# The third mixer of a two-block transformer kernel: value chunks ahead of query and key, with 1/rms spread inside the first query chunk

## What is computed

```python
# end of the first block
x = rmsnorm(x, final_norm_g)
# start of the second block
h = rms_norm(x, g_pre_mix)
proj = h @ w_in
mq, mk, mv, rq, rk, rv, rg = jnp.split(proj, SPLIT_POINTS, axis=-1)
mq = rotary(split_heads(mq, MOBA_HEADS), moba_inv, ROPE_DIM)
mk = rotary(split_heads(mk, MOBA_HEADS), moba_inv, ROPE_DIM)
mo = merge_heads(moba_attention(mq, mk, split_heads(mv, MOBA_HEADS)))
```

## Time and profile before

| | us |
|---|---|
| median of 3 runs | 1480.52 (1479.03 to 1480.96) |
| profiled execution | 1478.86 |
| its span | 1477.0 |
| PE busy | 1452.9 |
| DVE busy | 828.9 |
| ACT busy | 687.7 |
| POOL busy | 43.2 |
| DMA | 177 GB/s over the span |

### The profile page before, as it was taken

One profiled execution on the slowest core, in us unless ns is written; L12 is line 12 of the kernel. 1 busy time (PEld: TensorE's weight loads), 2 busy tenths in 40 slices (PEclk: granted clock), 3 DMA queues, 4 the chain that ended last, 5 costly groups with the idle time before them and its releaser, 6 DMA issues.

```text
span 1477.0 us, 18731 instructions
## 1 busy us (share of the span) xinstructions
PE 1452.9 (98%) x7412; PEld 1224.2 (83%) x7412; DVE 828.9 (56%) x927; ACT 687.7 (47%) x899; POOL 43.2 (3%) x96
## 2 busy tenths in 40 slices
PE   8999999999999999999999999999999999899997
PEld 6888889988888888888888788888787989788886
DVE  5655565865454555455666464554865565554454
ACT  6545445454444544435445455444544444544442
POOL 1000000000000000000000000000100100000000
PEclk9999999999999999999999999999999999999999
DMA  9755554445555455554444346455433543255551
GB/s 356 260 193 189 181 177 166 171 154 213 178 196 190 152 203 196 189 184 169 171 143 143 114 173 254 174 197 180 176 115 114 189 168 143 100 199 199 181 191 57
DMA packets 38574, 262.14 MB, mean 177 GB/s; under 512 B 4288, under 2 KB 4544, under 8 KB 7648
## 3 DMA queue, kind: packets, MB, share of 16 engines
q1 hardware_dynamic: 37152, 252.85, 48.4%
q0 software_dynamic: 1344, 8.16, 1.4%
HBM read 259.95 MB, written 1.05 MB: 177 GB/s over the span
## 4 chain that ended last, share of the span: by engine, by line
PE 95%; ACT 1%; DVE 1%; SPq 1%; DMA 1%; issue 0%; POOL 0%; POOLq 0%; DVEq 0%; ACTq 0%
PE prod L1001 15%; PE prod L1003 15%; PE prod L1002 15%; PE acc L1001 9%; PE acc L1003 9%; PE acc L1002 9%; PE prod L995 4%; PE prod L996 4%; PE prod L997 4%; PE acc L1168 2%; PE aux L1031 2%; PE acc L1018 1%; DMA raw<-in_weights_dram 1%; PE acc L1187 1%; PE o_bank L1220 1%; ACT acts_h L1319 0%
## 5 line engine op out<-in xcount | busy, mean ns | idle before, releaser
L1489 DVE TENSOR_TENSOR w_lo<-raw,w_hi 128x2048 fp32r<-128x2048 f32 x235 | 538.2, 2291 | 341.3 <-ACT w_hi L1301 341.1
L1301 ACT CAST w_hi<-raw 128x2048 fp32r<-128x2048 f32 x235 | 448.0, 1907 | 293.6 <-PE acc L1003 177.3
L1001 PE MATMUL prod<-w_hi,acts_h 128*128 128x512 f32 x944 | 375.9, 398 | 2.5 <-DVE w_lo L1497 1.7
L1003 PE MATMUL prod<-w_hi,acts_l 128*128 128x512 f32 x944 | 368.8, 391 | 0.0
L1002 PE MATMUL prod<-w_lo,acts_h 128*128 128x512 f32 x944 | 368.4, 390 | 0.0
L1001 PE MATMUL acc<-w_hi,mix_h 128*128 128x512 f32 x600 | 236.7, 395 | 0.3 <-DVE small L1581 0.3
L1003 PE MATMUL acc<-w_hi,mix_l 128*128 128x512 f32 x600 | 233.8, 390 | 0.0
L1002 PE MATMUL acc<-w_lo,mix_h 128*128 128x512 f32 x600 | 233.5, 389 | 0.0
L1001 PEld LDWEIGHTS prod<-w_hi,acts_h 128*128 128x128 f32 x944 | 177.8, 188 | 42.9 <-issue 7.0
L1003 PEld LDWEIGHTS prod<-w_hi,acts_l 128*128 128x128 f32 x944 | 177.5, 188 | 37.7
L1002 PEld LDWEIGHTS prod<-w_lo,acts_h 128*128 128x128 f32 x944 | 177.9, 188 | 35.1 <-issue 0.5
(11 more groups left out here) (255 smaller groups left out, 1220.9 us busy)
## 6 DMA issues: line engine op xcount, KB each, us to landing
raw<-in_weights_dram SPq DMA_DIRECT2D x235, 1024.0 KB, 4.9
raw<-in_weights_dram SPq DMA_DIRECT2D x12, 256.0 KB, 6.6
work<-in_mem_dram POOLq DMA_DIRECT2D x2, 1024.0 KB, 13.4
grow<-in_gain_rows_dram POOLq DMA_DIRECT2D x4, 512.0 KB, 4.4
tabs<-in_tabs_dram POOLq DMA_DIRECT2D x1, 1696.0 KB, 9.4
work<-in_x_t_dram SPq DMA_DIRECT2D x4, 256.0 KB, 6.3
x_res<-in_x_dram SPq DMA_DIRECT2D x1, 1024.0 KB, 8.7
work<-in_mem_t_dram POOLq DMA_DIRECT2D x1, 1024.0 KB, 14.4
```

The lines of the kernel that those rows point to most:

```text
L1001: pe.matmul(out, still_hi, wh, start=first, stop=False, skip_group_check=True)
L1003: return pe.matmul(out, still_lo, wh, start=False, stop=last, skip_group_check=True)
L1301: act.copy(w_hi[:, c % RING], raw[:, c % RAW]).then_inc(hi_done, 1)
L1489: dve.tensor_tensor(w_lo[:, c % RING], raw[:, c % RAW], w_hi[:, c % RING].bitcast(F32), ALU.subtract).then_inc(lo_done, 1)
```

## The change

The third mixer begins with the two value chunks. They are still opened in the middle, with nothing between the halves. The query chunk follows, now opened, with the spread of 1/rms in its middle; then the memory preparation; then the key chunk with the rotation of the query in its middle; then the second query chunk with the rotation of the key in its middle, where heads 0 to 3 are marked ready. The slot behind that chunk is the first that makes scores; before, it was the one ahead of that chunk. Everything from the second key chunk on is written as before.

```diff
--- before.py
+++ after.py
@@ -586,16 +586,13 @@
             pl.ready(units)
         return go
 
-    pl.project(w, 0, "q", 0)
-    pl.project(w, 512, "k", 0, mid=lambda: pl.spread("x"))
+    pl.project_tokens(w, 1024, "v", 0, mid=lambda: None)
+    pl.ready_v(moba)
+    pl.project(w, 0, "q", 0, mid=lambda: pl.spread("x"))
     pl.mem_prep("g_mem", [4, 5, 6, 7], [8, 9, 10, 11], "mem2")
-    pl.rope("q", 0, "moba", pl.read - 1)
-    k_read = pl.read
-    pl.project_tokens(w, 1024, "v", 0, mid=lambda: None, between=lambda: pl.rope("k", 0, "moba", k_read))
-    pl.ready(moba[0:4])
-    pl.ready_v(moba)
-    end(slot)
-    pl.project(w, COLS, "q", 2, mid=slot)
+    q_read = pl.read
+    pl.project(w, 512, "k", 0, mid=lambda: pl.rope("q", 0, "moba", q_read))
+    pl.project(w, COLS, "q", 2, mid=roped_slot("k", 0, "moba", pl.read, moba[0:4]))
     end(slot)
     pl.project(w, 512 + COLS, "k", 2, mid=roped_slot("q", 2, "moba", pl.read))
     end(slot)
```

## The result

| | before | after |
|---|---|---|
| median of 22 runs each | 1479.25 us (1477.89 to 1480.96) | 1481.20 us (1477.76 to 1483.87) |
| profiled execution | 1478.86 | 1483.29 |
| its span | 1477.0 | 1481.5 |
| mean granted clock | 0.995 | 0.992 |

The ratio is 1.0014, with a 95% interval of 1.0008 to 1.0021: some 2 us slower, and within the 0.2% that were set as the bound. The medians differ by 2.0 us, the two profiled executions by 4.4. The instruction rows tell which part of that is the change.

What follows compares the result with a forecast made beforehand. TensorE, busy 98% of the span, was taken as the bound: -2.72 (old waits) + 3.1 (new wait) - 0.4 (switches) + 1.2 (clock) = +1.2 us, added to the median 1480.52 for 1481.7 us; range 1478.6 to 1484.0.

Steps and rivals of the forecast that it cites:

- What bounds it: Start of the third mixer: three PE waits of 0.19, 1.69 and 0.84 us, together 2.72, are all the change can remove directly.
- The hold of POOL: POOL's 1/rms chain: a step issued during DVE's w_lo ends with it; 1/rms at 1053.0 to 1053.3, against 1050.64 before.
- Opening as the cause: At v1: opening this chunk flushes k0's split ahead of v1's scaling on DVE, w_lo running from 1049.6 to 1051.9.
- The wait that takes the place of the old one: Ahead of q0: PE waits 3.1 us for its product bank, until DVE has scaled v's first half with 1/rms.
- The clock: Behind q0's wait: PE's granted clock likely falls to 0.50 for 3.4 us, costing 1.2 us (0 to 2.4).
- Switches: Between chunks and scores: two switches fewer and two waits fewer save 0.4 us (0 to 0.8).
- Rotations and scores: From q0's end to the first scores: DVE side 13.1 us, PE 13.6, so both rotations are ready 0.5 us early.
- rival C: DVE's queue between q0's end and the first scores is late; scores wait up to 2.3 us, 1484.0 us; chance 0.13.
- B: POOL isn't held in mid-chain: 1/rms at 1051.1, PE waits 1.75 us ahead of q0, 1479.1 to 1480.3 us; chance 0.20.
- D: 1/rms arrives under the value chunks and no wait replaces the old ones: -3.1 us, 1477.4 us; chance 0.06.

Runs made afterwards that it cites:

- own bank: Changed kernel, but q0's product goes to the idle accumulator bank acc3, not the product bank holding v's first half; 0.9976 of before, 1476.58 us median.
- the unopened kernel: Changed kernel, but the two value chunks are not opened in the middle; ran once, 1482.88 us.
- the later scores alone: Old order, but the slots behind the value chunk and in the middle of q2 are left out; ratio to before 0.9989.

## Why the prediction was right

The forecast was +1.2 us and a change of under 0.2%; measured were +2.0 at the median (0.14%), +1.7 in the stretch. The mechanism was the one forecast: the old waits went, and a longer one came ahead of q0, by the hold of POOL and the product bank. That the time of 1481.2 lies so near the 1481.7 that was given is in part luck: the step was too small by 0.5 to 0.8 us, and the median before came out 1.3 lower over 22 runs than over 3, so that the two misses took each other back.

Point by point:

* **What bounds it.** PE's waits, 2.72 us in all. Right in the main: taking all of them away (own bank) gave 3.38 us, 0.66 more. A wait costs more than its bracket says. In the earlier trace rows the last matmul ahead of the spread starts at 1048.74 and the spread at 1050.70, 1.96 us later; the bracket says 1.69 and a step at full speed is 0.12, so 0.15 us come on top. The first steps behind a wait are longer as well. Over the three waits PE's rows give some 0.6 us, an estimate.
* **The hold of POOL.** Right in place and size. 1/rms was to come 2.4 to 2.7 us later than before; after the first matmul it came at 1054.47 - 1040.09 = 14.38 instead of 1050.64 - 1038.73 = 11.91, so 2.47. Of these, 0.54 are the later first step (1049.29 - 1040.09 = 9.20 against 1047.39 - 1038.73 = 8.66) and 1.92 the hold. A w_lo that starts between two steps of the chain had no row then; now it has. The rule of the Trainium skill that was weighed there (GPSIMD Engine Reference, section Specifications) is borne out by the 2.11, 2.10 and 0.19 us of the same step.
* **Opening as the cause.** Wrong as a reason, with no effect on the sum: an unopened value chunk does the same, since each engine does the splits that are due when it reaches a chunk, before its own part.
* **The wait that takes the place of the old one.** 3.1 predicted, 3.34 measured. The chain to q0 was right: 15.31 us after the first matmul (1055.40 - 1040.09), where 1054.0 - 1038.73 = 15.27 was reckoned. PE was through v0 and v1 sooner, at 1055.40 - 3.34 = 1052.06, 11.97 after the first matmul and not 12.2, mostly since I charged the turning of x too high (1.0 for 0.79, the step from 1042.84 to 1043.63).
* **The clock.** 1.2 taken, 1.45 in the profiled execution, 2.7 in another execution with the same wait (the unopened kernel). This term was mis-sized: I thought a third of the slow stretch would lie in the wait, and all of it lay behind. The bound of 2.4 was too low for a single execution.
* **Switches.** -0.4 taken. 1.69 = -2.72 + 3.34 + 1.45 - 0.38 leaves 0.38 for them in the changed kernel, but that is a remainder; the later scores alone saved nothing beyond their wait. By the estimate above (some 0.6 us beside three brackets before, some 0.2 beside the one after) it goes with the waits that went, not with the slots: of the term's two reasons, switches fewer and waits fewer, the second holds.
* **Rotations and scores.** 0.5 us of room was reckoned; DVE's second rotation ended 0.15 us ahead of the first scores (1075.60 + 0.69 against 1076.44). They didn't wait, but rival C was nearer than I thought.
* **Rivals.** B fell (the hold is there), C didn't come. B's reasoning that DVE would still have to finish its split first was sound: by the estimate above, the wait without the hold would have been 3.34 - 1.14 = 2.2 us, where B had 1.75. D, the full gain, was reckoned at -3.1; it exists (-3.4), but needs the bank, which the change left as it was.

## What to carry to other kernels

A wait on a late value doesn't go when the work that needs it is moved behind other work; it moves to the next thing that the value holds up, here a PSUM bank that can only be freed with it. Look at what frees the bank that the next work writes, and give that work another bank if one is idle: that took all of the wait, with no change in the order of the engines that make the value. And before a long VectorE instruction like the w_lo subtraction here (2.3 us, two inputs in SBUF) is brought forward, look whether a short GpSimd chain is under way beside it.

## What the runs showed of the hardware

* The third step of POOL's chain, on 128 x 2 elements, takes 0.19 us alone and 2.1 us if DVE's w_lo subtraction (2.31 us) starts 0.26 us ahead of it, and then it ends 0.06 us behind the subtraction; the changed kernel and four of the experiments show it, and the two with the subtraction behind the scaling show 0.19.
* The fall of the granted clock behind a wait isn't a fixed price: after 3.34 us of waiting it lasted 3.3 us in one execution and some 6 us in another, of the unopened kernel; after 1.43 us of waiting, and after useless matmuls (2.9 us) with 0.53 us of waiting behind them, it didn't come. Useless matmuls in a wait can pay: here the stretch was 1.55 us shorter.
